# A hybrid decoder layer on one Trainium2 core: SyncE issues weight transfers ahead of parameters, state stores and x loads

## The reference, cut to what matters

```
h  = rms_norm(x, g_mix)
q, k, v, xb, yb, ga, gb = split(h @ w_in)
a  = attention(q, k, v) @ w_oa                     # three dilation groups
xc = b_conv + sum_j w_conv[j] * xcat[:, j:j+t]     # 4 taps over xb and 3 old rows
r  = sigmoid(xc @ w_rg_a + b_rg_a)                 # block-diagonal gates
i  = sigmoid(xc @ w_rg_i + b_rg_i)
log_a = 8 * r * log_sigmoid(lam)
h_t = exp(log_a) * h_(t-1) + sqrt(1 - exp(2 log_a)) * i * xc
b  = (h_t * gelu(yb)) @ w_ob
x += (sigmoid(ga) * a + sigmoid(gb) * b) @ w_o
x += relu(rms_norm(x) @ w_up)^2 @ w_down
x += sigmoid(rms_norm(x) @ w_ple_gate) * (p @ w_ple_in)
```

## Time and profile before

| what | value |
|---|---|
| median of the runs | 2558.14 us |
| profiled execution, its own time | 2558.24 us |
| its span, first to last instruction | 2556.4 us |
| TensorE busy / VectorE / ScalarE / GpSimd | 2338.3 / 946.8 / 639.8 / 648.6 us |
| TensorE, share of the chain that ended last | 51% |
| DMA, share of 16 engines' span (main queue) | 18.3% |

### The profile page before, as it was taken

The page is one execution under the profiler, slowest core; times in us unless marked ns, Lnnn a source line. Parts: engine busy times, 40 slices in busy tenths (PEclk is TensorE's granted clock), DMA queues, the critical chain, the costliest instruction groups (busy, mean ns, idle before and its releaser), DMA issues.

```text
span 2556.4 us, 34085 instructions
## 1 busy us (share of the span) xinstructions
PE 2338.3 (91%) x13651; PEld 2307.4 (90%) x13651; DVE 946.8 (37%) x1624; ACT 639.8 (25%) x1383; POOL 648.6 (25%) x470
## 2 busy tenths in 40 slices
PE   2798998998999881999999999999999999999999
PEld 0798998998999871989999999999999999999999
DVE  6345346336434525577710113341112011112344
ACT  3231232233223220455611112221011011011331
POOL 1231113013112102333221212334234134233421
PEclk7898999899999965999999999999999999999999
DMA  3122222221212211111111111211111111111112
GB/s 112 54 79 103 78 68 75 94 79 56 92 63 79 78 53 62 38 39 39 53 44 49 67 50 59 84 58 48 46 44 47 49 42 50 42 42 67 50 42 85
DMA packets 60812, 156.98 MB, mean 61 GB/s; under 512 B 8628, under 2 KB 30011, under 8 KB 57543
## 3 DMA queue, kind: packets, MB, share of 16 engines
q1 hardware_dynamic: 60648, 154.71, 18.3%
HBM read 140.19 MB, written 16.86 MB: 61 GB/s over the span
## 4 chain that ended last, share of the span: by engine, by line
PE 51%; DVE 5%; ACT 1%; DMA 1%; issue 1%; SPq 0%; POOL 0%; ACTq 0%; DVEq 0%
PE d_ps L1193 51%; DMA w_raw<-w_stream 1%; DVE xc L1537 1%; DVE xc L1539 1%; DVE tmp L1556 1%; DVE tmp L1568 1%; PE d_ps L1208 0%; DVE act_lo L1598 0%; ACT L1303 0%; DVE ra L1550 0%; DVE zt L1572 0%; DVE tmp L1559 0%; DVE ri L1547 0%; ACT b_hi L1327 0%; ACT w_hi L1268 0%
## 5 line engine op out<-in xcount | busy, mean ns | idle before, releaser
L1468 POOL TENSOR_TENSOR w_lo<-w_raw,w_hi 128x1024 fp32r<-128x1024 f32 (+1 forms) x130 | 311.9, 2399 | 784.3 <-ACT w_hi L1268 784.3
L1193 PE MATMUL d_ps<-act_lo,w_hi 128*128 128x352 f32 x1728 | 375.8, 325 | 65.9 <-POOL w_lo L1468 58.5
L880 PE MATMUL at_proj<-qkv_hi,act_lo 128*128 128x384 f32 x864 | 344.9, 399 | 96.7 <-DVE qkv_lo L702 96.7
L1193 PE MATMUL d_ps<-act_hi,w_hi 128*128 128x352 f32 x1728 | 374.9, 325 | 0.0
L1193 PE MATMUL d_ps<-act_hi,w_lo 128*128 128x352 f32 x1728 | 372.8, 324 | 0.0
L1193 PEld LDWEIGHTS d_ps<-act_lo,w_hi 128*128 128x128 f32 x1728 | 299.1, 190 | 67.3 <-POOL w_lo L1468 58.8
L880 PE MATMUL at_proj<-qkv_hi,act_hi 128*128 128x384 f32 x864 | 331.1, 383 | 0.0
L880 PE MATMUL at_proj<-qkv_lo,act_hi 128*128 128x384 f32 x864 | 330.4, 382 | 0.0
L880 PEld LDWEIGHTS at_proj<-qkv_hi,act_lo 128*128 128x128 f32 x864 | 238.9, 277 | 98.6 <-issue 56.2
L1193 PEld LDWEIGHTS d_ps<-act_hi,w_hi 128*128 128x128 f32 x1728 | 296.1, 190 | 0.0
L1193 PEld LDWEIGHTS d_ps<-act_hi,w_lo 128*128 128x128 f32 x1728 | 294.3, 188 | 0.0
(11 more groups left out here) (216 smaller groups left out, 2566.9 us busy)
## 6 DMA issues: line engine op xcount, KB each, us to landing
w_raw<-w_stream SPq DMA_DIRECT2D x122, 512.0 KB, 3.3
qkv_raw<-w_qkv SPq DMA_DIRECT2D x12, 1536.0 KB, 6.5
vcache<-vc SPq DMA_DIRECT2D x12, 1024.0 KB, 5.0
kcache<-kc SPq DMA_DIRECT2D x16, 512.0 KB, 4.0
e_bc<-lse_dram SPq DMA_DIRECT2D x15, 528.0 KB, 5.5
x_in<-x_t SPq DMA_DIRECT2D x8, 528.0 KB, 7.8
tmp<-x_t SPq DMA_DIRECT2D x8, 528.0 KB, 3.9
kcache<-kc SPq DMA_DIRECT2D x16, 256.0 KB, 2.6
```

The lines of the kernel that those rows point to most:

```text
L880: ins = pe.matmul(pj[i % 3][:, 0:3 * HD], tile_cols(x, k, g, i), w[:, k], start=first, stop=last)
L1193: ins = pe.matmul(ps[s][:, c, 0:CH], w[:, u % 2, k0 + k], x[:, k, c * CH:(c + 1) * CH], start=k == 0 and x is lo, stop=k == nk - 1 and w i ...
L1468: pool.tensor_tensor(w_lo[:, s, 0:n], w_raw[:, s, 0:n], w_hi[:, s, 0:n].bitcast(F32), ALU.subtract).then_inc(S["wlo"], 1)
```

## The change

Three things are changed, all in `dense`. In the recurrent branch SyncE issues the weights of xb(m) and yb(m) one behind the other, and only then the state store (now that of m-3) and `load_lru(m)`. The parameters get four buffers instead of two; `load_lru` waits only from m = 4 on, for `save` and `rows` of four blocks before, and no longer for `z`. At W_o `load_x(m-1)` stands behind the weights of wo(m), and the last one behind those of up0. The other lines only follow the new buffer index.

```diff
-    prm = in_last("lru_prm", [P, 2, 39])
+    prm = in_last("lru_prm", [P, 4, 39])
...
         def load_lru(m):
-            y = m % 2
-            sp.wait_ge(S["save"], BUMP + m - 1)
-            sp.wait_ge(S["z"], BUMP + m - 1)
-            sp.wait_ge(S["rows"], BUMP + m - 1)
-            sp.dma_start(prm[:, y], a["lru_prm"][m]).then_inc(S[f"prm{y}_loaded"], 16)
+            y = m % 4
+            if m >= 4:
+                sp.wait_ge(S["save"], BUMP + m - 3)
+                sp.wait_ge(S["rows"], BUMP + m - 3)
+            sp.dma_start(prm[:, y], a["lru_prm"][m]).then_inc(S[f"prm{m % 2}_loaded"], 16)
             sp.wait_ge(S["ghi"], BUMP + m)
             sp.wait_ge(S["glo"], BUMP + m)
             sp.dma_start(g_raw[:], a["w_gates"][m]).then_inc(S["g_loaded"], 16)
...
         for u in range(NU):
             name, m = units[u]
             load_w(u)
-            if name == "xb":
+            if name == "yb":
+                if m >= 3:
+                    store_state(m - 3)
                 load_lru(m)
-            if name == "yb" and m >= 2:
-                store_state(m - 2)
+            if name == "gb" and m == 0:
+                store_state(KD - 3)
             if name == "bo" and m < 2:
                 store_state(KD - 2 + m)
             if name == "ga" and m == 1:
                 load_att()
-            if name == "wo":
-                load_x(m)
+            if name == "wo" and m:
+                load_x(m - 1)
+            if name == "up" and m == 0:
+                load_x(KD - 1)
```

More of the change, by code:

```diff
@@ L1273, in evict_xb @@
             act.wait_ge(S["cv"], BUMP + 4 * m)
-            act.activation(xcat_s[:, :, 0:3], seq(prm[:, y, 7:31]), ACT.Copy)
+            act.activation(xcat_s[:, :, 0:3], seq(prm[:, m % 4, 7:31]), ACT.Copy)
             act.wait_ge(S["mm"], mm_of("xb", m))
@@ L1526, in convolve @@
         def convolve(m):
-            y, out = m % 2, xc[m % 2]
+            y, out = m % 4, xc[m % 2]
             w = prm[:, y, 3:7]
@@ L1531, in convolve @@
             dve.wait_ge(S["init"], BUMP + 1)
-            dve.tensor_scalar(hb[:, y], prm[:, y, 1:3], 0.5, None, ALU.mult).then_inc(S["half"], 1)
+            dve.tensor_scalar(hb[:, m % 2], prm[:, y, 1:3], 0.5, None, ALU.mult).then_inc(S["half"], 1)
             dve.tensor_scalar(out[:, 0:NP_], xcat[:, 0:NP_], w[:, 0:1], prm[:, y, 0:1], ALU.mult, ALU.add)
@@ L1555, in recur @@
             first = seq(G[0][:, NP_:T])[:, :, 0]
-            dve.tensor_tensor(tmp8[:], first, prm[:, y, 31:39], ALU.mult).then_inc(S["h0m"], 1)
+            dve.tensor_tensor(tmp8[:], first, prm[:, m % 4, 31:39], ALU.mult).then_inc(S["h0m"], 1)
             dve.wait_ge(S["root_b"], BUMP + m + 1)
```

## The result

The changed kernel takes 2532.62 us (median of 4 runs, 2531.83 to 2538.3) against 2557.11 for the kernel before; the ratio is 0.9896, with a 95% interval from 0.9881 to 0.9910 (the two medians alone would give 0.9904, inside it). The forecast was 2530.6, with a range of 2527 to 2540. Its profiled execution took 2531.83 us with a span of 2530.0.

What follows compares the result with a forecast made beforehand. TensorE was taken to be held by waits for the gelu and act_lo, with late weight transfers one step behind. From 2558.2 us, minus 20.3 (branch) and 7.8 (W_o), plus 0.5 (start), gives 2530.6 us; range 2527 to 2540.

Steps and rivals of the forecast that it cites:

- The branch: Recurrent branch: the weight wait goes, blocks fall from 30.6 to TensorE's loop of 27.2 us; 20.3 us less.
- What became late next: Branch: TensorE's loop bounds at 27.22 us; VectorE and ScalarE's loop, with GpSimd's split on it, takes 26.8, reserve 0.4.
- Half clock: Branch: TensorE's half clock behind its pauses goes with them; granted clock stays at 1.00 to the branch's end.
- State stores: Branch: the later state store, landing 1.5 to 3.4 us after save, stays hidden, reserve 1.4 us at worst.
- rival 4: Branch: state stores land late, beyond the 4.8 us allowed, delaying rows, tanh and yb; kernel slower; chance 0.04.
- The start: Start of the dense part: the second weight transfer directly behind the first slows it; +0.5 us, between 0 and 1.3.
- W_o: W_o: wo1 no longer waits behind load_x; TensorE's 6.11 us pause falls to 0 to 1.1; gain 7.8 us.
- Sum: Whole kernel: 2558.2 - 20.3 - 7.8 + 0.5 = 2530.6 us.

Runs made afterwards that it cites:

- e1: Changed kernel with W_o's old order (load_x(m) behind wo(m)), so only the branch is changed; 2540.79 us, ratio 0.9908 to the kernel before.
- e5: Changed kernel, but GpSimd waits for z (end of the block's recurrence) before its half of yb's split; 2534.28 us, ratio 0.9901 to the kernel before.
- e6: Changed kernel, but ScalarE and GpSimd split xb(m+1) behind the gates' weights instead of ahead of the gates' tanh; 2529.26 us, ratio 0.9873.
- e3: Changed kernel with two parameter buffers and load_lru's old waits, the new order kept; 2538.44 us, ratio 0.9900 to the kernel before.
- the repetition: The changed kernel run once more, unaltered, in a later group; 2533.80 us, ratio 0.9904 to the kernel before.
- e8: Changed kernel with GpSimd's yb split behind z, xb's split behind the gates' weights, GpSimd's wo1 split behind all of u; 2526.40 us, ratio 0.9871.
- e4: Changed kernel with SyncE's old order in the branch, four buffers and load_lru's new waits kept; 2532.89 us, ratio 0.9886 to the kernel before.
- e9: Changed kernel with two buffers and load_lru's old waits, state store of m-2 ahead of the parameters; 2532.01 us, ratio 0.9896.
- e2: Kernel before with only W_o's order changed, the branch as before; 2552.22 us, ratio 0.9949 to the kernel before.

## Why the prediction was right

**The branch.** 20.3 us forecast. 183.63 - 163.38 = 20.25 in the traces, 19.9 by e1. TensorE's loop of 27.22 was measured as 27.23. The last block of the kernel before was a faithful model of all blocks after.

**What became late next.** GpSimd's half of the split falls on VectorE's recurrence, 2.26 us for 8 elements in seven of the eight blocks, as forecast; e5 and e6 show that it is real, hidden, and one step from being the bound. The loop of VectorE and ScalarE is 27.0 (e6) and not 26.8, so the reserve was 0.25 us and not 0.4. Part of this is a reading: the prediction counted the way from the gelu to the next `half_bias` from the start of the gate product at 1235.45 (1.1 us), while the gelu itself ended at 1234.26 + 1.05 = 1235.31 (1.2 us).

**Half clock.** It went with the pauses: 1.00 through the branch.

**State stores.** Hidden in the changed kernel, landing in 1.5 us throughout. My reasons against rival 4 were right for this kernel. But the rival was nearer than its chance of 0.04 said: the landing times of 3.4 us at most were read from a kernel in which the store followed one weight transfer. In block 4 of e3 it was issued 1.9 us after `save` (raised at 1132.12) behind two, and `rows` had it at 1138.23, 6.1 us after `save`, where rival 4 allowed 4.8. That is 1.3 us too much, and TensorE's pause grew by 1.2 (1.84 against 0.63).

**The start.** +0.5 forecast. The first transfer landed in 3.50 us against 3.44, so sharing cost 0.06. TensorE did reach block 1 0.6 us later, counted from its first matmul (41.29 against 40.70), with about one and a half more groups of matmuls at half clock; in the repetition it took 40.59. So the 0.6 us are not an effect of the change, and the forecast's +0.5 did not appear as such.

**W_o.** 7.8 forecast. Before, 8.4 us were lost; now the sixth group starts at 1575.87 where 1571.84 + 6 x 0.487 = 1574.76 would be possible, 1.1 lost. Gain 7.25, 6.9 by e1: at or just under the lower end of the range of 7.3 to 8.4. GpSimd took its turn in front of the small splits of u and delayed everything behind them by its 2.4 us; without that turn (e8) there is no pause.

**Sum.** 20.25 + 7.25 - 0.6 = 26.9 against 1541.8 - 1515.0 = 26.8 us in the dense stage. The forecast had 27.6. By the medians the changed kernel is 24.5 us faster, by the ratio 23 to 30 us; the time came out 2.0 us above the forecast. That the sum of the parts meets the dense stage within 0.1 us is partly luck, since the dense stage of the same kernel differed by 0.6 us between two executions.

Where I was misled was the cause, not the size: I followed the edit and spoke of weights issued ahead of the parameters. e4 shows that the removed wait of `load_lru` is enough, in either order, and e9 that the order is enough without it, if the state store stands ahead. My text told only of the order. By itself, with the store behind two weight transfers, that is e3, which is 8.7 us slower than the changed kernel.

## What to carry to other kernels

In a queue that issues all transfers, look for the one transfer that waits for something late, and ask what stands behind it: removing its wait by a few hundred bytes of buffer can do more than reordering the queue, and holds in more orders. Where a stage is repeated, look for the one repetition that already lacks the stall; its rows give both loops and what will be late next. A small store that someone waits for should not go out behind large loads.

## What the runs showed of the hardware

Half clock (1.2 GHz) came behind pauses of TensorE of 1.84 us (e3) and of 2.36 and 2.47 us (e2), and did not come behind one of 2.59 us. One execution of the kernel before shows both sides: the pause below, 2.58 us, was followed by half clock (0.50 from 1115 to 1117 us).

```profile
1112.74 0.73 PE L1220 MATMUL d_ps<-xc_lo,g_hi 128*128 128x352 f32 x3 [2.58 <-ACT tmp L1303]
```

So the length of a pause alone does not tell. The kernel before and e2, whose branch has the same code, differ by 1.8 us there; the three kernels without such pauses (changed kernel, e1, e4) agree in their spacing within 0.02 us.

An instruction of VectorE that waits for GpSimd shows as a long instruction (2.26 us for 8 elements, 0.17 when GpSimd is held back in e5), not as idle time, so no view of waits names it. Another such row was there all along: the 8-element product just before (L1556 before, L1560 after) takes 2.4 us in seven of eight blocks of both kernels, beside GpSimd's `conv_lo`. No run moved that one. An 18 KB store landed in 1.5 us with no weight transfer just ahead, 3.2 (median) behind one 512 KB transfer, and 4.1 behind two.
